# Narrow sums placed a few at a time between tiles of broad products, in a float32 program of two model blocks

## The reference, cut to what matters

```python
u = rms_norm(h, norm_mix_g[i])
proj = u @ w_in[i]
q1 = rms_norm(q[..., 0, :], q_norm_g[i])      # per head of 64, also q2, k1, k2
...
hl = modulate(x, norm1_g[i], sh1, sc1)        # rmsnorm(x) * (1 + scale) + shift
cq, ckv, kr, gq, gk, gv = jnp.split(z, ATTN_SPLITS, axis=-1)
q = (rmsnorm(cq, q_a_g) @ w_q_b).reshape(B, L, MLA_HEADS, MLA_NOPE + MLA_ROPE)
```

## Time and profile before

| | |
|---|---|
| median of three runs | 3148.76 us (3146.38 to 3149.04) |
| the profiled execution's own time | 3151.97 us |
| its span, first to last instruction | 3150.0 us |
| mean granted clock of TensorE | 0.995 |
| busy: TensorE, its weight loads, VectorE, ScalarE, GpSimd | 99%, 81%, 63%, 39%, 20% |

### The profile page before, as it was taken

How to read it: one execution, slowest core, us unless ns; L and a number is a source line. 1 busy time by engine, 2 the same in 40 slices (tenths; PEclk the granted TensorE clock), 3 DMA queues, 4 the chain that set the end, 5 groups by cost and what they waited for, 6 DMA issues and landing times.

```text
span 3150.0 us, 36124 instructions
## 1 busy us (share of the span) xinstructions
PE 3118.6 (99%) x14782; PEld 2536.1 (81%) x14782; DVE 1977.0 (63%) x2664; ACT 1228.2 (39%) x1653; POOL 615.7 (20%) x479
## 2 busy tenths in 40 slices
PE   9999999999999999999999999999999999999998
PEld 7877788888888777888888866788888888888887
DVE  7555666666666457567766657766555589963333
ACT  4234433323432344422235355644433453352222
POOL 1000010000200010499991010012333101010001
PEclk9999999999999999999999999999999999999999
DMA  3222233455222222355533001023332422322221
GB/s 127 84 94 81 81 145 143 150 211 187 94 81 89 82 87 94 104 192 194 190 139 126 27 19 40 15 86 132 114 130 101 160 94 94 108 94 98 103 94 67
DMA packets 55620, 342.38 MB, mean 109 GB/s; under 512 B 5984, under 2 KB 7840, under 8 KB 18208
## 3 DMA queue, kind: packets, MB, share of 16 engines
q1 hardware_dynamic: 54080, 337.46, 29.9%
q10 hardware_dynamic: 1376, 2.62, 0.2%
HBM read 327.47 MB, written 12.58 MB: 108 GB/s over the span
## 4 chain that ended last, share of the span: by engine, by line
PE 79%; POOL 10%; DVE 6%; ACT 2%; issue 2%; DMA 0%; POOLq 0%; ACTq 0%; DVEq 0%
PE PS L264 78%; POOL FA L273 10%; ACT PB L270 1%; PE PS L267 1%; DVE FA L281 1%; DVE PB L273 1%; DVE wl L273 1%; DVE UL L273 1%; DVE PS L273 1%; DVE SC L273 0%; ACT SC L270 0%; DVE UL L281 0%; DVE FA L273 0%; DVE ST L293 0%; ACT FA L270 0%
## 5 line engine op out<-in xcount | busy, mean ns | idle before, releaser
L264 PE MATMUL PS<-UH,wh 128*128 128x512 f32 (+1 forms) x2120 | 837.4, 395 | 2.2 <-DVE wl L273 0.7
L264 PE MATMUL PS<-UH,wl 128*128 128x512 f32 (+1 forms) x2120 | 824.4, 389 | 0.0
L264 PE MATMUL PS<-UL,wh 128*128 128x512 f32 (+1 forms) x2120 | 824.3, 389 | 0.0
L273 DVE TENSOR_TENSOR wl<-raw,wh 128x2048 fp32r<-128x2048 f32 (+2 forms) x255 | 563.0, 2209 | 390.7 <-ACT wh L270 390.6
L264 PE MATMUL PS<-RH,wh 128*128 128x512 f32 (+2 forms) x1640 | 642.9, 392 | 0.9 <-DVE wl L273 0.9
L264 PE MATMUL PS<-RH,wl 128*128 128x512 f32 (+2 forms) x1640 | 637.8, 389 | 0.0
L264 PE MATMUL PS<-RL,wh 128*128 128x512 f32 (+2 forms) x1640 | 637.5, 389 | 0.0
L270 ACT ACTIVATE wh<-raw 128x2048 fp32r<-128x2048 f32 (+2 forms) x255 | 452.7, 1780 | 245.3 <-DMA raw<-in_wall 165.7
L264 PEld LDWEIGHTS PS<-UH,wh 128*128 128x128 f32 x2120 | 400.5, 189 | 105.1 <-issue 17.8
L264 PEld LDWEIGHTS PS<-UL,wh 128*128 128x128 f32 x2120 | 400.7, 189 | 83.4 <-issue 3.8
L264 PEld LDWEIGHTS PS<-UH,wl 128*128 128x128 f32 x2120 | 400.3, 189 | 83.2
(11 more groups left out here) (218 smaller groups left out, 3071.0 us busy)
## 6 DMA issues: line engine op xcount, KB each, us to landing
raw<-in_wall SPq DMA_DIRECT2D x224, 1024.0 KB, 4.8
FA<-in_wmod SPq DMA_DIRECT2D x48, 1024.0 KB, 4.9
raw<-in_wall SPq DMA_DIRECT2D x29, 512.0 KB, 3.6
kspec<-FA SPq DMA_DIRECT2D x8, 1024.0 KB, 6.9
FA<-kspec SPq DMA_DIRECT2D x8, 1024.0 KB, 6.8
PB<-in_window SPq DMA_DIRECT2D x16, 256.0 KB, 4.5
Hs<-in_xT ACTq DMA_DIRECT2D x4, 512.0 KB, 8.0
FA<-in_w SPq DMA_DIRECT2D x4, 512.0 KB, 5.7
```

What stands on the lines that cost most here:

```text
L264: return self.put(self.eng and self.eng.matmul(out, w, x, start=start, stop=stop, skip_group_check=True))
L273: return self.put(self.eng and self.eng.tensor_tensor(out, a, b, op))
```

## The change

The order of TensorE's instructions changes; no other engine's list does. In both layers only the first head sum stays where it was; the other three follow the 2nd, 4th and 6th product of tile 6. The second attention's norm sums go position block by position block behind products 6 and 7 of the second context tile and products 0 and 1 of the third (their bank is taken one step earlier). The latent queries' sums go behind products 4 to 7 of `gq(0)`.

```diff
+        def square_sum(n, i):
+            p.wait_ge("ssq", (n, 6))
+            p.wait_ge("h_sq", (n, 7))
+            out = ps(("ms", n))[:, i:i + 1]
+            p.matmul(out, SSQ[:, 128 * i:128 * i + 128], ones[:, 0:1], True, False)
+            p.matmul(out, scr(("sq", n, 7))[:, 128 * i:128 * i + 128], ones[:, 0:1], False, True)
+            if i == 3:
+                p.then_inc("sum", ("ms", n))
...
-                    for x in range(4):
-                        head_sum(l, x)
+                    head_sum(l, 0)
                     continue
                 for m, k in enumerate(ks):
                     key = ("qk", l, k)
                     take(key, ("qk_x", (l, k)))
-                    group(key, ps(key), [(pair(("qk", l, i), 256 * t + 128 * m), U(t), u_made(n, t)) for t in range(8)])
-                    for x in ((0, 1), (2, 3), (4, 5), (6,))[k - 4]:
+                    for t in range(8):
+                        three(ps(key), pair(("qk", l, i), 256 * t + 128 * m), U(t), t == 0, t == 7)
+                        if t == 7:
+                            p.then_inc("sum", key)
+                        elif m == 0 and t % 2:
+                            head_sum(l, 1 + t // 2)
+                    for x in ((4, 5), (6,))[m]:
                         head_sum(l, x)
...
-        def both(tag, key, o, stride=256):
+        def both(tag, key, o, sums={}):
...
+            for k in range(8):
+                p.wait_ge("c_lo", k)
+                three(ps(key + (0,), NC), pair(tag, 256 * k + o), C(k), k == 0, k == 7)
+                if k == 7:
+                    p.then_inc("sum", key + (0,))
+                if k in sums:
+                    square_sum(6, sums[k])
...
             both(kv, ("kv", 0), 0)
-            both(kv, ("kv", 1), 128)
-            square_sums(6)
-            both(gk, ("gk",), 0)
+            take(("ms", 6), ("rs", 6))
+            both(kv, ("kv", 1), 128, {6: 0, 7: 1})
+            both(gk, ("gk",), 0, {0: 2, 1: 3})
...
+                for i in range(8):
+                    three(ps(("gq", k)), pair(("gq", k // 2), 256 * i + 128 * (k % 2)), U(i), i == 0, i == 7)
+                    if i == 7:
+                        p.then_inc("sum", ("gq", k))
+                    if k == 0 and i >= 4:
+                        latent_query_sum(i - 4)
```

More of the change, by code:

```diff
@@ L990, in context_sum @@
             p.then_inc("sum", ("ctx",))
-        def both(tag, key, o, stride=256):
+        def both(tag, key, o, sums={}):
             p.wait_ge("w_lo", tag)
             take(key + (0,), ("a_in", key + (0,)))
-            group(key + (0,), ps(key + (0,), NC), [(pair(tag, stride * k + o), C(k), [("c_lo", k)]) for k in range(8)])
+            for k in range(8):
[5 more added lines that the diff above has]
+                    square_sum(6, sums[k])
         def job_sum(key, lhs, width, squares):
@@ L1040, in gq, with latent_query_sum @@
                 take(("gq", k), ("j_sq", ("q", k)))
-                group(("gq", k), ps(("gq", k)), [(pair(("gq", k // 2), 256 * i + 128 * (k % 2)), U(i), u_made(6, i)) for i in range(8)])
+                for i in range(8):
[4 more added lines that the diff above has]
+                        latent_query_sum(i - 4)
             def gq_turn(k):
                 turned(("q", k), fat(GQ, k), 128, "rotG", [("a_in", ("gq", k)), ("ld_c2", 0)])
-            def latent_query_sums():
+            def latent_query_sum(i):
                 for m in range(3):
                     p.wait_ge("j_sq", ("c", m))
[L1049 to L1052, removed]
+                    p.matmul(ps(("rq",), 1, o=32 + i), query_square(("c", m))[:, 128 * i:128 * i + 128], ones[:, 0:1], m == 0, m == 2)
+                if i == 3:
+                    p.then_inc("sum", ("cs",))
             def query_sums(k):
@@ L1093, in second_attention @@
             gq(0)
-            latent_query_sums()
             gv_turn()
```

## The result

The changed kernel takes 3152.05 us (median of 22 runs, 3146.93 to 3157.70) against 3147.31 us before (22 runs, 3145.41 to 3150.03): +4.7 us between the medians. The ratio that is taken over all runs is 1.0017 with a 95% interval of 1.0011 to 1.0023, or +3.5 to +7.2 us. So it is a little slower, and most of that interval lies inside the 0.2% that the prediction called about as much as can be told. The runs also scatter over 10.8 us where they scattered over 4.6. The profiled execution took 3154.08 us with a span of 3152.1; that of before had taken 3151.97, which is above every one of its 22 timed runs. That turned out to matter.

A forecast was written before the change was run, and what follows sets the result against it. TensorE, busy for 99% of the span, was taken to bound the kernel. Layer 0 +6.8, layer 1 -3.1, norm sums +0.7 and latent sums -1.0 gave +3.4 us on 3148.76: 3152.2 us, range 3145.0 to 3156.5.

The forecast's parts named there:

- The likeliest case: Whole kernel: terms +6.8, -3.1, +0.7 and -1.0 us give 3152.2 us, +0.11%; chance 0.55.
- The wait in layer 0: Layer 0, first product of tile 6: TensorE stands idle for `wl` until 54.06 us, 3.2 us.
- How long the clock stays low: Layer 0, tile 6: the unknown, with tile 6 ending +2.4 us later at the lower bound, +6.3 at the upper.
- the upper case: Layer 0: clock low while narrow groups interrupt broad matmuls, +6.3 us, +8.0 with the float32 sums; +6.8 taken.
- Layer 1: Layer 1's head sums: no wait for `wl`, clock holds, gain 3.2 us; -3.1 taken.
- The worry about VectorE's later reading: Layer 1: VectorE reads the sums later, leaving less slack ahead of the next weights; -3.1 taken from a 3.2 us gain.
- Norm sums: Second attention: wait of 1.3 us for `wl`, likely followed by a clock fall; +0.7 us taken.
- the bound "+0.7 to +1.6": Second attention, third context tile: its later end in us if the clock falls as before, 0.51 for 3.4 us.
- Latent sums: Latent queries' sums: 0.3 us wait for the square, gain 1.0 us if the clock holds, 0.6 lost otherwise; -1.0 taken.
- No gain from splitting a run: All places: eight narrow passes cost 0.90 us wherever they stand at full clock; the skill's rule would gain about 0.3 each.
- Rival 3: Layer 1: clock falls though sums are spread, +3.3 us in place of -3.1, sum +9.8, 3158.6 us; chance 0.13.

The follow-up runs named there:

- the early weights: The changed kernel with ScalarE rounding the high part of layer 0's weights i = 3 ahead of its squares of heads: 3144.09 us against 3146.47 before.
- the place timed alone: The kernel before with only layer 0's head sums spread: 3154.66 us against 3146.83, ratio 1.0023.
- the closest pair of profiles: All four places spread, layer 0's weights rounded early, norm sums ahead of their wait (3142.93 us), and the same with layer 1's sums together (3144.94 us); before 3146.47.
- latent-only kernel: The kernel before with only the latent queries' sums spread: 3146.16 us against 3146.83, ratio 1.000.
- part-by-part runs: The kernel before with one place spread at a time, against 3146.83 us: layer 1 3147.03, layer 0 3154.66, norm sums 3148.89, latent sums 3146.16.

## Why the prediction was right

The likeliest case came true: 3152.2 us forecast, 3152.05 measured. The closeness is partly luck, for its parts erred both ways (+6.8, -3.1, +0.7 and -1.0 forecast; +5.6, -1.8, +1.4 and -0.7 by the mean stretches), and it was added to a median of three runs that 22 runs put 1.4 us lower; the move was +4.7 and not +3.4.

- *The wait in layer 0*: 3.2 us forecast, 3.06 measured, and shown as its cause by the early weights.
- *How long the clock stays low.* Taken from the upper case, "no row shows the clock rising while narrow groups stand in it". It stayed low for 10 us and returned inside the third group, a little sooner. The place's term was +6.8; the two profiles give +4.6, the two spread stretches against the mean of five together +5.2 and +6.0, the place timed alone +7.8 with an interval of 4.1 to 10.4 that holds all of them.
- *Layer 1*: -3.1 forecast and -3.2 between the profiles, but -2.0 in the median. The step that failed is "Before, 897.66 to the end of tile 6 at 909.94: 12.3 us". It took one execution's low clock for the kernel's, whose mean over seven profiles is 10.9. The worry about VectorE's later reading cost nothing in the closest pair of profiles (806.30 and 806.31 us, above).
- *Norm sums*: +0.7 forecast, +2.5 between the profiles, +2.1 alone. The wait was right (1.3, measured 1.36). In the changed kernel's profile the low clock lasted twice as long as the bound "+0.7 to +1.6" allowed, 6.83 us in place of 3.4. In the three other profiles with the same sums the fall came later and the place took 13.15 to 13.42 us, +0.6 to +0.9 against the 12.52 of before, which is the forecast's term. So here too one profile is one draw; why the fall comes sooner in one of them, no run shows. Also, VectorE now waited for the sums (0.96 us), which was told as 0.6.
- *Latent sums*: -1.0 forecast, -1.2 between profiles, -0.7 alone and -0.7 between the mean stretches; the wait for the square 0.23 us (forecast 0.3).
- *No gain from splitting a run*: by the rule of the Trainium skill that the prediction cites (TensorE: Matmul & The Clock Gate, "Architectural detail: the array is 16× 32×32, not 1× 128×128"), weight loads pulled ahead of matmuls in flight would have made each place some 0.3 us cheaper, as the prediction estimated. Layer 1's spread stretch is 9.11 us and the same work together at the full clock 9.03 (latent-only kernel), so splitting even costs 0.08 us; the measurement decides against that gain here.
- *Rival 3*, that the clock falls in layer 1 though the sums are spread, is refuted by all six profiles that have them spread.
- Missed altogether: that runs would scatter more. The change traded costs of 0 to 3 us for a wait that brings a longer low clock, whose length also differs between executions. The medians of the part-by-part runs don't add up (7.8 + 0.2 + 2.1 - 0.7 = 9.4 against 4.7), but each has an interval of some 3 us to either side, and the mean stretches add up to 4.5; nothing here shows that the parts act on each other.

## What to carry to other kernels

Before moving work from in front of a wait to behind it, read when the awaited thing is ready: work that fills a wait is free. Moved behind it, it is paid in full, since the wait ends no sooner, and the idle stretch that it leaves can bring a low clock on top. Move the producer first. And where a cost is a fall of TensorE's clock, one profile tells only that it can occur; compare the profiled execution's time with the timed runs, and look at the same untouched place in several profiles before pricing it.

## What the runs showed of the hardware

- The same 32 narrow passes of layer 1 (3.5 us at full clock) were followed by no low clock in two profiles, by 3.4 us of it in two and by 6.8 us of it in three, though the code is equal there. The fall can come within the run (899.90) or 1.2 us behind it (902.49), when broad work has begun.
- Groups of eight narrow passes between six broad matmuls of 512 columns left the clock at 2.4 GHz in six of six profiles of layer 1. Behind 3.06 us of idleness in layer 0 (3.05 in the second profile), with the same groups following, the clock fell to 1.2 GHz and stayed there for 10 us (some 13.6 in the second, from within the wait on). With that stretch filled by broad matmuls, or the wait cut to 0.47 us, it did not fall in that place.
- Twenty-four narrow passes and six transposes (3.2 us) brought the low clock in four of six profiles and left it full in two.
- Narrow passes at half the clock take 1.56 us for eight (56.09 to 57.65), at the full clock 0.81 (902.44 to 903.25).
